# Sixteen cache copies beside a decoder layer: three of them leave the query and key stage and go out in parts in the feed-forward, and a semaphore clear moves

## The reference

```python
h = rms_norm(x, norm1_g) * (1 + sc1) + sh1
q, k, v, u = split(h @ w_in)                  # then q and k are RMS-normed head by head
...
k_all = jnp.concatenate([cache_k_l, k.astype(cache_k_l.dtype)], axis=1)
v_all = jnp.concatenate([cache_v_l, v.astype(cache_v_l.dtype)], axis=1)
parts = [dilated_cached(q, k_all, v_all, rel_bias, w, d, n_hist) for (w, d) in DILATED_PATTERNS]
return combine_dilations(parts), k_all[:, -n_hist:], v_all[:, -n_hist:]
...
x = x + g2 * (jnp.square(jax.nn.relu(h2 @ w_ff1)) @ w_ff2)
```

## Time and profile before

| | |
|---|---|
| median of 3 executions | 2605.22 us (2602.17 to 2607.79) |
| the profiled execution | 2604.63 us, of it 2602.8 us from the first to the last instruction |
| TensorE (PE) busy | 2515.0 us, 97% of the span |
| VectorE (DVE), GpSimd (POOL), ScalarE (ACT) busy | 72%, 50%, 49% |
| DMA | 507.84 MB, mean 195 GB/s |
| granted TensorE clock, mean | 0.985 of 2.4 GHz |

### The profile page before, as it was taken

How to read it: one execution, slowest core, us unless ns; L and a number is a source line. 1 busy time by engine, 2 the same in 40 slices (tenths; PEclk the granted TensorE clock), 3 DMA queues, 4 the chain that set the end, 5 groups by cost and what they waited for, 6 DMA issues and landing times. The chain is left out here.

```text
span 2602.8 us, 46423 instructions
## 1 busy us (share of the span) xinstructions
PE 2515.0 (97%) x16058; PEld 2231.9 (86%) x16058; DVE 1879.3 (72%) x4104; ACT 1281.9 (49%) x3185; POOL 1306.6 (50%) x920
## 2 busy tenths in 40 slices
PE   7999999899999889999899999999999999999998
PEld 4788867687777646887899999999999999999998
DVE  4268898797999647877866666666767786667776
ACT  3443324457888624655434443434555554455553
POOL 0000006006999205664655555556777775677773
PEclk8999999899999999999999999999999999999999
DMA  7866524953445794664456666665555657565443
GB/s 300 289 215 236 205 97 161 302 154 117 136 138 163 271 351 154 190 216 139 150 179 250 235 242 228 211 215 164 183 191 178 193 182 237 167 198 159 144 141 126
DMA packets 362197, 507.84 MB, mean 195 GB/s; under 512 B 29338, under 2 KB 277894, under 8 KB 352102
## 3 DMA queue, kind: packets, MB, share of 16 engines
q1 hardware_dynamic: 340090, 455.45, 53.2%
q0 software_dynamic: 4272, 39.19, 4.3%
q10 hardware_dynamic: 17604, 10.24, 1.3%
HBM read 405.10 MB, written 171.81 MB: 222 GB/s over the span
## 5 line engine op out<-in xcount | busy, mean ns | idle before, releaser
L3159 POOL TENSOR_TENSOR ff_w_lo<-gluT,ff_w_hi 128x512 fp32r<-128x512 f32 x450 | 626.7, 1405 | 319.2 <-ACT ff_w_hi L3217 317.1
L3217 ACT ACTIVATE ff_w_hi<-gluT 128x512 fp32r<-128x512 f32 x450 | 278.7, 626 | 271.6 <-PE ff_u_ps L3685 168.6
L3683 PE MATMUL ff_u_ps<-ff_a_hi,ff_w_hi 128*128 128x352 f32 (+1 forms) x696 | 223.4, 321 | 3.7 <-POOL ff_a_lo L3175 2.5
L3685 PE MATMUL ff_u_ps<-ff_a_hi,ff_w_lo 128*128 128x352 f32 (+1 forms) x696 | 223.0, 320 | 0.0
L3684 PE MATMUL ff_u_ps<-ff_a_lo,ff_w_hi 128*128 128x352 f32 (+1 forms) x696 | 222.5, 320 | 0.0
L1810 ACT ACTIVATE pa_score<-pa_score,pa_stat 128x256 f32<-128x256 f32 (+1 forms) x384 | 172.3, 451 | 30.2 <-DVE pa_stat L1752 27.9
L3683 PE MATMUL ff_u_ps<-ff_h_hi,ff_w_hi 128*128 128x352 f32 (+1 forms) x548 | 176.0, 321 | 1.6 <-DVE ff_u L3567 0.8
L3685 PE MATMUL ff_u_ps<-ff_h_hi,ff_w_lo 128*128 128x352 f32 (+1 forms) x548 | 175.2, 320 | 0.0
L3684 PE MATMUL ff_u_ps<-ff_h_lo,ff_w_hi 128*128 128x352 f32 (+1 forms) x548 | 174.9, 319 | 0.0
L307 DVE SCALAR_TENSOR_TENSOR vu_dwp<-gluT,tapT,vu_dwp 128x512 f32<-128x512 f32 x240 | 161.1, 750 | 0.8 <-DVE rstd L215 0.8
L1025 PE MATMUL vu_z_ps<-vu_w_hi,last_hi 128*128 128x512 f32 (+1 forms) x384 | 152.0, 396 | 0.7 <-DVEq L963 0.7
(11 more groups left out here) (565 smaller groups left out, 7735.3 us busy)
## 6 DMA issues: line engine op xcount, KB each, us to landing
gluT<-in_w_ff_dram SPq DMA_DIRECT2D x196, 256.0 KB, 3.5
gluT<-in_w_ff_dram SPq DMA_DIRECT2D x64, 512.0 KB, 5.2
gluT<-tu_d SPq DMA_DIRECT2D x112, 256.0 KB, 3.5
gluT<-td_d SPq DMA_DIRECT2D x96, 256.0 KB, 3.2
out_new_k_sample_dram<-in_cache_k_dram SPq DMA_DIRECT2D x40, 511.0 KB, 5.2
out_new_v_sample_dram<-in_cache_v_dram SPq DMA_DIRECT2D x40, 511.0 KB, 5.6
dwq<-in_w_ada_dram SPq DMA_DIRECT2D x32, 512.0 KB, 9.3
gluT<-in_cache_k_dram SPq DMA_DIRECT2D x16, 1024.0 KB, 8.7
```

What stands on the lines that cost most here:

```text
L3159: pool.tensor_tensor(slot_view(w_lo, s), src, slot_view(w_hi, s).bitcast(F32), ALU.subtract).then_inc(w_lod, 1)
L3217: act.activation(slot_view(w_hi, s), src, ACT.Copy).then_inc(w_hid, 1)
L3683: pe.matmul(out, w_hi[s % WR][:, w], hi, start=first, stop=False, skip_group_check=more)
L3685: return pe.matmul(out, w_lo[s % WR][:, w], hi, start=False, stop=last, skip_group_check=more)
```

## The change

The constant falls from 6 to 3, so three copies go whole (all in the `vu_` stage) and thirteen in parts, 104 instead of 80. The three copies of the query and key stage are gone from GpSimd's list. In runs 1 and 2 of the feed-forward a part is issued at every fourth slot of a block instead of every sixth, which makes room for 47 per run. Apart from that, the feed-forward's `clear_ended()` moves from ahead of the block into GpSimd's own list, behind its first weight slot and the four low parts of the activations. The final waits count from the same constant and need no edit.

```diff
-        COPIES_AHEAD, COPY_PARTS = 6, 8
+        COPIES_AHEAD, COPY_PARTS = 3, 8
@@ queries and keys, GpSimd
                         pool.sem_inc(dw_done, 1)
-                        for i in (2, 5, 8):
-                            pool.wait_ge(z_pe, 2 * i)
-                            copy_cache(pool, 3 + i // 3)
@@ feed-forward, ahead of the block
-            clear_ended()
             with nc.Block() as block:
@@ feed-forward, SyncE
                         load_slot(s)
-                        if blk and i % 6 == 3:
+                        if blk and i % 4 == 3:
                             next_part()
@@ feed-forward, GpSimd
                     low(1)
                     h_low(0, 3)
+                    clear_ended()
                     for s in range(2, WR):
                         low(s)
```

## The result

| | before | after |
|---|---|---|
| median of 4 executions each, on one chip | 2603.69 us (2602.16 to 2607.79) | 2587.98 us (2586.83 to 2589.47) |
| ratio after / before, 95% interval | | 0.994 (0.9925 to 0.9955) |
| profiled execution, its span | 2604.63, 2602.8 us | 2586.83, 2585.0 us |

The change makes the kernel 0.6% faster. The medians differ by 15.7 us where 13.2 were forecast. The kernel before was run again beside the experiments, which went over three chips: 2601.44 us (17 executions, experiments 1 to 3 and the clear alone), 2601.24 (11, experiments 5 to 7 and the copies alone) and 2601.03 (13, experiment 8). Each experiment's ratio is taken against the kernel before on its own chip. The changed kernel was not run again there; against 2601.44 its gain would be 13.5 us.

What follows compares the result with a forecast made beforehand. TensorE, busy 2515.0 of 2602.8 us, was taken as the bound, so time could come only from its waits or lower clock. From 2604.63 us, -13.7 + 0.0 + 0.5 = -13.2 gave 2591.5 us, range 2587 to 2598.

Steps and rivals of the forecast that it cites:

- the sum: Whole kernel: -13.7 + 0.0 + 0.5 = -13.2 us against the profiled execution's 2604.63, so 2591.5 us.
- The bound, and the chain behind the wait: Query and key stage: TensorE bounds; two whole copies delay SP's store of keys, then ScalarE's copy, so TensorE waits 10.8 us.
- the second wait: End of the query and key stage: TensorE's 4.24 us wait at 605.92, after the copies' traffic has ebbed, stays.
- Part 1: Query and key stage: the three copies leave, saving 13.7 us, about 11.0 of wait and 2.7 of the next period.
- VectorE as the next one late: Query and key stage: VectorE is nearest to being late, 17.89 of 20 us busy, 10% left, and follows TensorE.
- Part 2: Feed-forward: 24 more parts cost 0, within bounds of 0 and 65 us; DMA rate 188 to 209 GB/s.
- Part 3: Feed-forward entry: the moved clear pushes back GpSimd's second slot and costs 0.5 us, between 0 and 0.8.
- The sign: Feed-forward: TensorE's wait for GpSimd's second slot moves from 1245.62 to about 1232 and grows from 0.44 to about 1 us.
- D: Query and key and next stage: less traffic around 500 brings loads sooner, 3 to 6 us more, 2586 to 2588; 3%.
- Rival A: Query and key stage: SP's long list leaves a wait of 5 to 10 us, 2597 to 2602 us; 8%.
- Rival B: Query and key stage: wait is SP's own; equal queue turns at most double a store to 11.4 us; 2605.2 us; 6%.
- Rival C: Feed-forward, runs 1 and 2: extra parts make weight slots late; at 1 us each, 2615.5 us; 3%.

Runs made afterwards that it cites:

- experiment 1: Kernel before with the three whole copies of the query and key stage left out and nothing in their place: 2587.23 us, ratio 0.9949.
- experiment 2: Kernel before with the same three copies cut into pieces of 4088 bytes (8,176-byte packets): 2633.18 us, ratio 1.012.
- experiment 3: Kernel before with the three whole copies waiting for tiles 6, 9 and 12 instead of 2, 5 and 8: 2588.13 us, ratio 0.995.
- the clear alone: Kernel before with only the feed-forward's clear moved behind GpSimd's first weight slot and four low parts: 2601.65 us, ratio 1.0.
- experiment 5: Kernel before with all three whole copies of the query and key stage issued together (tiles 2, 3 and 4): 2611.35 us, ratio 1.0041.
- experiment 6: Kernel before with the three copies as 24 parts issued by SP in the query and key stage, two per tile: 2588.87 us, ratio 0.9952.
- experiment 7: Changed kernel with a part at every second weight slot instead of every fourth: 2589.2 us, ratio to the kernel before 0.9948.
- the copies alone: Changed kernel with the clear put back ahead of the feed-forward's block: 2588.27 us, ratio to the kernel before 0.9949.
- experiment 8: Kernel before with the three copies in half-way packets of 16,352 bytes: 2599.72 us, ratio 0.9995.

## Why the prediction was right, point by point

The forecast of 2591.5 us stands against 2587.98, inside the range of 2587 to 2598 and 1 us from its lower end. No term of the sum accounts for the 3.5 us between them. The gains that were measured side by side with the kernel before, in experiments 1, 3, 6 and 7 and with the copies alone, are 12.0 to 14.2 us, close to the 13.2 of the sum. But the sum starts from 2604.63, some 3 us above the kernel before in its later executions (2601.0 to 2601.4). So the gain was met, and the time itself is within scatter of the edge.

- **The bound, and the chain behind the wait.** Right. The 10.8 us went in every run in which no two whole copies go together (left out, spaced, or cut into parts), and in none in which they do; the second wait, 4.2 us at the stage's end, stayed in the changed kernel as said.
- **Part 1, 13.7 us.** Measured 13.3 from the stage's own ends. Starts of transposes were the right measure: the wait alone, 10.8, would have missed what the lower clock took behind it. VectorE as the next one late: it was busy for up to 19.40 of 20 us (19.10 from 440 to 460 in the kernel before) and TensorE didn't wait for it, so "10% left", read from one window, was too much.
- **Part 2, 0.** Right: 0.1 us over 1349.7, and twice the density does nothing either. The rate was forecast as 209 GB/s and came out as 204, since the sum took all 73 parts into the 617 us and 67 fell in them. The old 49 parts do not stand behind the same slots any more, as the prediction's "in the same places" can be read; it did no harm.
- **Part 3, 0.5 us.** GpSimd's gap is 0.76 us where the medians of the two instructions gave 0.53; 0.23 us of it is neither of them. TensorE's wait grew by 0.48 (0.44 to 0.92), as forecast. Whether the program pays that is below what eleven traces can separate. The sign put that wait at about 1232; it came at 1227.76, by what the untouched stretches gave.
- **The sum, -13.2.** The steps themselves give -13.3 + 0.1 + 0.8 = -12.4 by the trace, of which the last term is within scatter. The other 5.3 us between the profiled executions lie in stretches that the change doesn't touch. The 2.5 us by which the medians' 15.7 exceeds the forecast may be no more than scatter: on one chip the copies alone give 13.0 (2601.24 - 2588.27). It is not D: experiments 3 and 6 gain the same, 13.3 and 12.4 us, with copies' traffic around 500.
- **Rival A** fell: no rest of the wait. SP's list alone makes no wait of TensorE: its longest issue in the stage is 1.6 us in the changed kernel, where it was 14.62.
- **Rival B** fell, as held likely, but its working was wrong in a way that matters. It took equal turns to mean that a store takes at most twice its time, 11.4 us. Turns are equal in packets, not in bytes or time. A turn of 65 KB against one of 2 KB makes equal turns a starvation, and the store took 26.7. The prediction also said that the trace doesn't agree with the rule as a bound; it is the inference of "at most twice" that fails; the rule itself is what the counts show in the first stretch of each run with copies together.
- **Rival C** fell, with room to spare: landings of up to 7.6 us at twice the density, against a cover of 9.45. The order within SP's queue, a part ahead of the next weights, shows as 0.3 us more in the median, and 1.1 more again at twice the density, and ends there.

## What to carry to other kernels

Before moving background traffic, look at what a wait of TensorE follows back to: here it was not the bytes in a window (254 GB/s in the same stage do no harm) but two whole DRAM-to-DRAM copies under way at once on one queue, while another queue needed many small packets on time. Look at packets per microsecond of the queues beside GB/s, and at when the last copy lands. Space large copies so that each one's landing lies within the slack of the buffers, or cut them into separate DMAs that are issued a few at a time (here on the queue that would otherwise wait); cutting the packets of one DMA smaller did not help. A stall is priced by the distance of starts over it, since the lower clock behind it was a fifth of the cost here.

## What was not expected of the hardware

- Two queues got the same number of packets within some 15% while copies were issued together (126 to 110, 192 to 185, 329 to 331, 540 to 599), so a queue of small packets can fall to a thirtieth of the bytes (0.23 MB against 7.19). In the later stretch of the small packets it was 290 to 1074.
- A store on one queue landed 0.2 to 1.3 us behind the last copy of another, at three packet sizes, 26.7 to 46.2 us after its own issue. Equal turns alone don't explain the longest of these.
- A smaller packet made a DRAM-to-DRAM copy slower, and much so between 16 and 8 KB: alone 18.1 and 29.3 us for the same 4088 KB, against 16.3 in the large packets of the kernel before. The 16 KB packets hardly changed the wait (11.5 us against 10.8) and not the time of the kernel.
- A single DMA issue on SP can be held for 14.62 us when its queue doesn't move, although those ahead of it take 0.33 to 0.74 us.
- A drain and a clear in the middle of GpSimd's work leave a gap of 0.76 us, more than their own two durations.
